# Two-layer-pair transformer in float32 on one Trainium2 core: residual with tokens on partitions, output projections with stationary tokens

## What is computed

```python
h = x
for layer in range(2):                       # first_block
    hn = rmsnorm(h, norm_mix_pre[layer])
    mix = gmlp_shortconv(hn, ...) if layer == 0 else dilated_attention(hn, ...)   # ends in @ w_out / @ w_o
    h = h + rmsnorm(mix, norm_mix_post[layer])
    f = square(relu(rmsnorm(h, norm_mlp_pre[layer]) @ w_up)) @ w_down             # 2048 -> 8192 -> 2048
    h = h + rmsnorm(f, norm_mlp_post[layer])
for layer in range(2):                       # second block
    hn = rms_norm(h, pre_norm_w[layer])
    mix = concat(diff_attention, sliding_window_attention, latent_attention)(hn @ w_in) @ w_out
    h = h + rms_norm(mix, post_norm_w[layer])
```

## Time and profile before

| | |
|---|---|
| Time, median of 3 runs | 3035.4 us (3034.12 to 3035.45) |
| The profiled execution's own time | 3034.49 us |
| Its span, first to last instruction | 3032.7 us |
| Mean granted clock of TensorE | 0.998 |
| PE busy | 3011.0 us, 99% |
| DVE, ACT, POOL busy | 71%, 48%, 10% |
| DMA | 549.49 MB, mean 181 GB/s, 50.3% of the 16 engines' time |

### The profile page before, as it was taken

The page is one execution under the profiler, slowest core; times in us unless marked ns, Lnnn a source line. Parts: engine busy times, 40 slices in busy tenths (PEclk is TensorE's granted clock), DMA queues, the critical chain, the costliest instruction groups (busy, mean ns, idle before and its releaser), DMA issues.

```text
span 3032.7 us, 42068 instructions
## 1 busy us (share of the span) xinstructions
PE 3011.0 (99%) x17482; PEld 2643.9 (87%) x17482; DVE 2167.7 (71%) x2878; ACT 1461.9 (48%) x1834; POOL 292.0 (10%) x191
## 2 busy tenths in 40 slices
PE   8999999999999999999999999999999999999999
PEld 7888888888888888888888888888888888888888
DVE  6776765767666687765856667676789865889764
ACT  5334534434334565445533334334666545656554
POOL 0003300000000410004100000002400003200003
PEclk9999999999999999999999999999999999999999
DMA  6555455555555444445455555555444445444445
GB/s 257 190 184 189 161 193 189 187 193 188 188 194 185 178 179 167 179 158 200 164 188 194 186 189 195 184 191 193 170 165 170 164 153 181 168 180 153 157 154 190
DMA packets 77500, 549.49 MB, mean 181 GB/s; under 512 B 8576, under 2 KB 9088, under 8 KB 11520
## 3 DMA queue, kind: packets, MB, share of 16 engines
q1 hardware_dynamic: 77312, 546.81, 50.3%
HBM read 544.68 MB, written 2.10 MB: 180 GB/s over the span
## 4 chain that ended last, share of the span: by engine, by line
PE 50%; DVE 2%; ACT 0%; issue 0%; DVEq 0%
PE acc L314 28%; PE acc L321 14%; PE score L546 1%; PE acc L839 1%; PE acc L364 1%; DVE w_low L1364 1%; PE head_out L575 1%; PE acc L846 1%; PE acc L374 1%; PE score L554 0%; PE acc L403 0%; PE acc L392 0%; PE extra L475 0%; ACT swapped L1049 0%; DVE y L1380 0%
## 5 line engine op out<-in xcount | busy, mean ns | idle before, releaser
L924 ACT ACTIVATE w_high<-raw 128x2048 fp32r<-128x2048 f32 x511 | 974.5, 1908 | 1109.8 <-DMA raw<-stream 1109.2
L1364 DVE TENSOR_TENSOR w_low<-raw,w_high 128x2048 fp32r<-128x2048 f32 (+1 forms) x509 | 1163.7, 2287 | 150.1 <-ACT w_high L924 147.1
L314 PE MATMUL acc<-xs,w_high 128*128 128x512 f32 x4444 | 1081.4, 394 | 0.6 <-ACT w_high L924 0.6
L314 PEld LDWEIGHTS acc<-xs,w_high 128*128 128x128 f32 x4444 | 819.6, 188 | 170.0 <-issue 6.9
L314 PE MATMUL acc<-inner,w_high 128*128 128x512 f32 x2880 | 679.9, 391 | 0.0
L314 PEld LDWEIGHTS acc<-inner,w_high 128*128 128x128 f32 x2880 | 532.7, 188 | 105.6 <-issue 0.7
L321 PEld LDWEIGHTS acc<-xs,w_low 128*128 128x128 f32 x4450 | 568.6, 192 | 17.0 <-issue 1.6
L321 PE MATMUL acc<-xs,w_low 128*128 128x256 f32 x4450 | 582.1, 283 | 1.3 <-DVE w_low L1364 1.3
L1380 DVE TENSOR_REDUCE y<-acc 128x256 f32<-128x512 f32 x374 | 258.0, 690 | 419.3 <-PE acc L321 247.0
L321 PEld LDWEIGHTS acc<-inner,w_low 128*128 128x128 f32 x2976 | 372.6, 191 | 9.7 <-issue 0.2
L321 PE MATMUL acc<-inner,w_low 128*128 128x256 f32 x2976 | 375.6, 283 | 0.1
(11 more groups left out here) (197 smaller groups left out, 1619.0 us busy)
## 6 DMA issues: line engine op xcount, KB each, us to landing
raw<-stream SPq DMA_DIRECT2D x514, 1024.0 KB, 4.8
out<-finished SPq DMA_DIRECT2D x8, 256.0 KB, 2.0
h<-x_t SPq DMA_DIRECT2D x3, 512.0 KB, 10.0
consts<-tables SPq DMA_DIRECT2D x1, 960.0 KB, 16.2
h<-x_t SPq DMA_DIRECT2D x2, 256.0 KB, 4.7
raw<-stream SPq DMA_DIRECT2D x2, 256.0 KB, 5.6
raw<-stream SPq DMA_DIRECT2D x1, 512.0 KB, 6.7
branch<-w_spatial SPq DMA_DIRECT2D x1, 512.0 KB, 17.0
```

Source lines behind the costliest of these rows:

```text
L314: return nc.tensor.matmul(acc[s if bank is None else bank][:, :], w_high[:, s, kt * P:(kt + 1) * P], x[:, kt, :, :], start=(kt == first_of ...
L924: nc.scalar.activation(w_high[:, s, 0:units * P], raw[:, s, 0:units * P], ACT.Copy)\
L1364: V.tensor_tensor(w_low[:, s, 0:units * P], raw[:, s, 0:units * P], w_high[:, s, 0:units * P], ALU.subtract).then_inc(low_ready, 1)
```

## The change

1. `h` and `branch` have tokens on partitions (`[P, TB, D]`). The input is loaded twice: features on partitions as `x_in` for the first sublayer, tokens on partitions into `h` later.
2. All output projections (`w_out`, `w_down`, `w_o`, 12 groups of 16 chunks, 192 chunks) and the first four chunks of both MLPs' up projections become wide chunks (`both_halves`, `one_half`, L377): stationary `inner` or `xs`, 512 moving weight columns. The last group of a sublayer ends with chunks 2 and 3 for the first 128 tokens, then for the second (`half_done` after the first).
3. Sums of squares run along the free dimension: ACT squares with an accumulator (`post_square`, `pre_square`). POOL only makes roots. The post gain is 512 columns of DVE (`out_gain`) with a gain row that SP loads, 4 pieces of 256 KB for each sublayer.
4. `turn_rows`: for each sublayer but the last 8 groups of 4 transposes by PE bring the new `h` back to features on partitions; ACT and DVE make `xs` from PSUM in pieces of 128 x 128 (`passage`). The next sublayer's first four chunks (`input_group`) follow the order in which they come (`TURNS`). In each MLP `turn_up` adds two groups of four.
5. `product_first`, `wide_first`, `parted`, `add_parts`, `product_last`, `product_low_first`, 17 `column_sums`, the 5 `spread`s of post-norm roots and the transposes at the end are gone. `h` is written out directly.

```diff
+TURNS = [(0, 0), (0, 1), (1, 0), (1, 1), (0, 2), (1, 2), (0, 3), (1, 3)]    # (half of the tokens, group of 4 blocks)
...
 # SP
+                for m, first in enumerate(OUTPUTS):
+                    g = c - 3 - first
+                    if 0 <= g < GROUPS:
+                        sp.dma_start(gain[:, wide_cols(g)], gains_post[m, :, wide_cols(g)])\
+                            .then_inc(sem(f"gain_landed_{g}"), 16)
...
 # PE
+            def one_half(c, i, n, x, banks, order=NATURAL, ready=None, hooks=None):
+                for k, (w, part) in enumerate(((w_high, 0), (w_high, 1), (w_low, 0))):
+                    pe.wait_ge(low_ready if w is w_low else high_ready, c + 1)
+                    for a in range(KT_WIDE):
+                        if hooks and KT_WIDE * k + a in hooks:
+                            hooks[KT_WIDE * k + a]()
+                        if ready and w is w_high:
+                            ready(KT_WIDE * i + a, part)
+                        mm = wide_unit(w, c % 4, x, order[KT_WIDE * i + a], a, part, n, banks[n], ...)
+            def turn_rows(m, k):
+                n, j = TURNS[k]
+                pe.wait_ge(sem("h_ready"), FINAL_GROUPS * m + k + 1)
+                if k > 2:
+                    pe.wait_ge(sem("xs_ready"), inputs_at(m + 1, k - 3))
+                for b in range(KT_WIDE):
+                    mm = nc.tensor.transpose(turn_banks[k % 3][:, b * P:(b + 1) * P],
+                                             h[:, n, (KT_WIDE * j + b) * P:(KT_WIDE * j + b + 1) * P], ident)
+            def input_group(c, n, banks, out0):
+                one_half(c, 0, 0, xs, banks, ready=first(0))
+                one_half(c + 1, 1, 0, xs, banks, ready=first(0), hooks={1: lambda: turn_rows(m, 2)})
+                one_half(c, 0, 1, xs, banks, ready=first(1), hooks={1: lambda: turn_rows(m, 3)})
+                one_half(c + 1, 1, 1, xs, banks, ready=first(1),
+                         hooks={4: lambda: turn_rows(m, 4), 8: lambda: turn_rows(m, 5)})
+                both_halves(c + 2, 2, xs, banks, ready=second,
+                            hooks={5: lambda: turn_rows(m, 6), 7: lambda: turn_rows(m, 7)})
+                both_halves(c + 3, 3, xs, banks, ready=second)
...
 # ACT, passage: high = rounding of a chunk, turn(k) = 4 copies of 128 x 128 to xs's high part
+                high(c, 0); last_sum(0); high(c + 1, 1); turn(0); turn(1); last_sum(1); turn(2)
+                high(c + 2, 2); pre_square(0); pre_square(1); turn(3); high(c + 3, 3); turn(4)
+                pre_square(2); turn(5); pre_square(3); high(c + 4, 0); turn(6); pre_square(4); turn(7)
...
 # DVE, passage: low = w_low of a chunk, add(k) = 512 columns of h, xs_low(k) = 4 of 128 x 128
+                low(c, 0); last_rows(0); add(0); add(1); xs_low(0); xs_low(1); last_rows(1)
+                add(2); low(c + 1, 1); add(3); xs_low(2); add(4); xs_low(3); add(5)
+                low(c + 2, 2); xs_low(4); add(6); xs_low(5); add(7); low(c + 3, 3); xs_low(6); xs_low(7)
```

More of the change, by code:

```diff
@@ L101, with inputs_before, build @@
 N_COLS = LAM_INIT + 2 * LAYERS
[L104 to L114, removed]
+def inputs_before(n):
+    return KB + TB * KB * (n - 1) if n else 0
+def build(nc, stream, x_t, x_rows, columns, gains_post, lambdas, w_spatial, b_spatial, positions, tables, out):
     ctx = ExitStack()
@@ new lines, in passage, with turn, pre_square @@
+            def passage(m, c, last_sum, gain_read):
+                def turn(k):
+                    n, j = TURNS[k]
+                    if j == GROUPS - 1:
+                        gain_read()
+                    act.wait_ge(sem("rows_turned"), FINAL_GROUPS * m + k + 1)
+                    for b in range(KT_WIDE):
+                        kt = KT_WIDE * j + b
+                        nc.scalar.activation(xs[:, kt, 0, rows(n)], turn_banks[k % 3][:, b * P:(b + 1) * P], ACT.Copy,
+                                             scale=column(G_PRE + KB * (m + 1) + kt)).then_inc(sem("xs_high"), 1)
+                def pre_square(k):
+                    n, j = TURNS[k]
+                    act.wait_ge(sem("h_ready"), FINAL_GROUPS * m + k + 1)
+                    act.wait_ge(sem("pre_squared"), FINAL_GROUPS * m + k)
+                    nc.scalar.activation(squares[:, :], h[:, n, wide_cols(j)], ACT.Square,
+                                         accum_out=pre_sums[:, n, j:j + 1]).then_inc(sem("pre_squared"), 1)
+                high(c, 0)
+                last_sum(0)
+                high(c + 1, 1)
+                turn(0)
+                turn(1)
+                last_sum(1)
+                turn(2)
+                high(c + 2, 2)
+                pre_square(0)
+                pre_square(1)
+                turn(3)
+                high(c + 3, 3)
+                turn(4)
+                pre_square(2)
+                turn(5)
+                pre_square(3)
+                high(c + 4, 0)
+                turn(6)
+                pre_square(4)
+                turn(7)
+                for k in range(5, FINAL_GROUPS):
+                    pre_square(k)
@@ L2087, in weight_stream @@
             blocks(w, part * width + P * j)
-    blocks(w_out_ab[0], 0, KB)
+    order = [r for b in MIX0_ORDER for r in range(P * b, P * (b + 1))]
+    for i in range(GROUPS):
+        wide(w_out_ab[0][order], WIDE * i)
     def mlp(layer):
         for q in range(FFN_QUARTERS):
-            blocks(w_up[layer], D * q, KB)
-            blocks(w_down[layer][D * q:D * (q + 1)], 0, KB)
+            if q == 0:
+                wide(w_up[layer], 0)
+                blocks(w_up[layer], WIDE, KB - KT_WIDE)
+            else:
+                blocks(w_up[layer], D * q, KB)
+            for i in range(GROUPS):
+                wide(w_down[layer][D * q:D * (q + 1)], WIDE * i)
     mlp(0)
@@ L2100, in weight_stream @@
                 blocks(w_qkv[0], D * part + P * hd)
-    blocks(w_o[0], 0, KB)
+    for i in range(GROUPS):
+        wide(w_o[0], WIDE * i)
     mlp(1)
@@ L2132, in weight_stream, with per_feature @@
         order += list(range(1536, D))
-        blocks(w_out_2[layer][order], 0, KB)
+        for i in range(GROUPS):
+            wide(w_out_2[layer][order], WIDE * i)
     return stream.reshape(LOADED, P, UNITS * P)
-def per_feature(sink_logits_2, gains_pre, gains_post, conv_w, q_norm, kv_norm, subln):
+def per_feature(sink_logits_2, gains_pre, conv_w, q_norm, kv_norm, subln):
     col = np.zeros((P, N_COLS), np.float32)
```

1032 lines of the change are left out of this document (454 added, 578 removed).

## The result

The changed kernel takes 3013.56 us (median of 4 runs, 3013.05 to 3015.66) beside 3034.76 us (3032.86 to 3035.45) for the kernel before on the same chip: a ratio of 0.9933, 95% interval 0.992 to 0.9945. It is faster by 0.7%. The forecast was 3020 us, range 3006 to 3033. The span of the profiled execution fell from 3032.7 to 3011.6 us, by 21.1 where the steps gave 15.4.

The account below looks back on a forecast made before the run. PE, busy 3011.0 of 3032.7 us, was taken as the bound. Terms -24 - 9.4 - 10.6 + 21 - 4.2 - 16.2 + 28 sum to -15.4 us, forecast 3020 us by the median, range 3006 to 3033.

Parts of the forecast that it names:

- (g): New passages between sublayers: PE waits for DVE and ACT, 5.2 us three times and 6.2 twice, +28 us.
- (d): Added PE transposes, 44 groups of four in `turn_rows` and `turn_up`, 0.48 us a group: +21 us.
- (f): Old PE waits at the passages go: 6.8 us into each MLP, 0.85 into three others, -16.2 us.
- (e): Kernel's end: last product to end falls from 11.5 to 7.3 us, half the rows leaving earlier, -4.2 us.
- (a): Projections and MLPs: 200 narrow chunks made wide, 5.44 instead of 5.56 us each, -24 us.
- (b): Products gone: double work of `parted` -8.2 us, short matmuls of six `product_last` -1.2 us.
- (c): 17 column sums and 5 spreads gone from PE's stream, 0.48 us a group, -10.6 us.
- Rival 5: Transposes run at the price of two-pass float32 matmuls: +15 us, 3035 us; chance 0.02.
- 1, the clock: PE's waits in the passages lower its clock, 8 us more each, 40 in all: 3060 us; chance 0.06.
- 2, the dearer passage: Passages cost about 9 us each without the clock, 45 in place of 28: 3037 us; chance 0.15.
- 3: Wide chunks bring nothing, (a) is 0: 3044 us; chance 0.04.
- 4, the better hidden passage: Overlap on DVE and ACT brings each passage to 2 to 3 us: 3006 us; chance 0.15.

Follow-up runs that it names:

- e1_short_pairs: Kernel before, with 16 matmuls of 256 columns in each narrow chunk's third pass made 8 of 512, same columns: 2989.17 us, ratio 0.9852.
- e15_sums_back: Changed kernel with 44 groups of two one-column sums, result unused, put among both MLPs' up products: 3034.27 us, 20.7 over the changed kernel.
- e4_no_unused_loads: Changed kernel without the three loads (3 MB) at the end of the stream that no product uses: 3010.79 us, ratio 0.992.
- e3_order: Changed kernel with the passage's DVE and ACT queues reordered, pieces PE waits for ahead of work that has time: 3005.38 us, ratio 0.9902.
- e13_whole_group: Changed kernel with each sublayer's last group not cut in halves and all its rows turned behind the last product: 3038.99 us, ratio 1.0015.
- e2_turn_twice: Changed kernel with each group of `turn_rows` transposes issued twice, 160 more transposes: 3022.43 us, ratio 0.9958 to the kernel before.

## Why the prediction was right

The mechanism was right, and the number partly by errors that cancel. The span fell by 5.7 us more than the sum said. The terms below come out 11.5 us cheaper ((g) 8, (d) 1.5, (f) 1.6, the start 0.4) and 3.9 us dearer ((e) 2.3, two sums 1.0, (a) 0.6), 7.6 in balance; the rest of 1.9, most of it as 0.4 to 0.8 in each of the three passages into a mixer, was not traced.

**(a) Chunks made wide: right.** -23.4 (12 groups of 16 at 1.87, of which six are measured alone in the middle of the MLPs, and 8 chunks at 0.117) for -24. e1_short_pairs gets the same 0.117 from the other layout, so the reason given, fewer matmuls for the same columns, is shown. The Trainium skill's rule for an isolated gap, columns / 2.4 + 2.5 ns ("TensorE: Matmul & The Clock Gate", section "Back-to-back issue gap"), would have made it an estimated -4; the section itself does not offer that rule for a stream, and these float32r matmuls in a stream start 226.7 ns apart, not 215.8. The prediction's "11 to 14 ns" over the columns' time is 13 to 14 by its own rows.

**(b), (c): right.** Neither `parted` nor a sum is left in the passages, and e15_sums_back measures 0.47 for the 0.48 a group. Two of the sums were counted twice, 1.0 us: they lay in the 11.5 us of (e). No run takes the double work of `parted` out alone.

**(d) Transposes: right, a little dear.** A group costs 0.36 and 0.08 to 0.1 behind it, 0.44 to 0.45 for 0.48, 1.5 us less in all. Rival 5 falls.

**(e) The end: mis-sized.** 9.6 us instead of 7.3. The chain was right (ACT's square 0.60 and 0.19 in place of 0.7, four adds in 2.74), the transfer was not: I took 2.1 us from the earlier trace rows, and it is 5.4 beside the last unused load. e4_no_unused_loads gives 2.1 and 7.0. The mean, 0.15 without a row, is 0.16. The prediction said that loads are no part of the passage and never asked about the loads at the end.

**(f) Waits of before: nearly right.** Two I had not looked for, 0.30 and 0.64 among the first narrow chunks behind `product_first` in each MLP (359.74 and 366.17 in the first), went as well (-1.9 together). The second MLP's idle stretch was 1.2 us shorter than the first's (1436.91 to 1441.50), but there the clock stood at 0.51 for 6 us of work instead of 4, about 0.9 us more lost, so 6.8 was 0.3 too much for it.

**(g) Waits of the new passage: right place, too dear.** About 3.3 us three times (the three waits named make 3.05 of it) and about 5 twice, 20 in all where I had 28. I put most of the surplus down to ACT and DVE on PSUM pieces, which no run isolates: four of 128 x 128 take 1.16 and 1.12 us, where I took 1.3 to 1.6 and 1.1 to 1.4, and a root 0.55 where I took 0.7. The timetable's waits add up to 4.6 and not to the 4.8 it says. It placed the third chunk's wait at 2.4 in sum and the fourth's at 1.65; they are 1.73 and 1.32. Its early waits of 0.25 and 0.3 do not exist in front of an MLP. Behind one they are 0.84 and 1.11 by the starts (0.68 and 0.95 in the brackets), where the timetable with 0.7 more for each has 0.95 and 1.0. That DVE's queue decides in front of the third chunk fits the rows of DVE above and e3_order, which takes `low` out of the way, reorders ACT a little too, and gets 8.2 us.

**Rivals.** 1, the clock: in all passages of the changed kernel it stays at full level, with waits of 1.5 us at most; e13_whole_group shows the danger to be real, since four of its five waits of 2.4 to 3.6 us are followed by a fall to 1.2 GHz. The Trainium skill says that a transpose does not count as PE-busy in the same way ("TensorE: Matmul & The Clock Gate", section "Part 4: PE-mode transpose"); eight groups of four among products, and eight groups of eight in e2_turn_twice, did not lower it in any passage. 2, the dearer passage: false, 4 us on the mean and not 9. 3: false. 4, the better hidden passage: true in direction, at 3.3 to 5 us and not 2 to 3. The time came out between the forecast's 3020 and its 3006.

**What I said would show it.** Wide chunks 5.44: yes. Transposes 0.09 us each, 160 of them: yes. Waits of 5 to 6 us in front of the third and fourth chunk: no, 3.05 into an MLP and 2.8 into the third sublayer, though ended by DVE and ACT as said. PEclk full: yes. 7 us at the end: only without the unused load. PE busy about 2990: 2979.

## What to carry to other kernels

Price a stream of matmuls by the distance of their starts in the trace, and count instructions as well as columns: here each, with its weight load, costs about 14 ns over its columns' time, and trading two of 256 columns for one of 512 was the whole gain in the projections. Where a chain between two stages can't be removed, cut the last stage so that half of the result is ready early. Then look at what stands ahead of the awaited pieces in the queues of the helping engines: moving the weights' `low` behind them was worth two fifths of the change again. At a program's end ask which transfers nobody waits for share the DMA engines with the output.

## What was not expected

- An idle stretch of 2.8 us on PE was followed by a fall of the clock and a loss of 1.7 us in the work behind it (0.51 over 330.5 to 334.0 in e13_whole_group); so was one of 2.44 us in the same kernel, and one of 2.45 was not.
- Outside the passages the clock can fall behind shorter waits, and not in every execution. In front of two groups of sums in the first sublayer PE waits 1.38 us in the changed kernel and 0.99 in e2_turn_twice, where the instructions up to this point are the same. Windows of the changed kernel and then of e2_turn_twice:

```profile
48.00:51.00 3.00, 3.00 (x14) 2.47 (x14) 1.09 (x2) 0.99 (x1) 1.76 (x2) 1.00 0.00 0
```

```profile
48.00:51.00 3.00, 3.00 (x9) 2.38 (x8) 0.45 (x2) 1.62 (x2) 1.75 (x2) 0.53 0.00 0
```

- The 256 KB writes at the end took 5.4 us (median) beside an unused 1 MB load and 2.1 us without it.
- Doubling the transposes cost half of their own time, since they ate a wait: 8.9 us for 17.4 us of work.
- The start of PE's first product varies between executions, 7.87 us in the profile of before, 6.83 in that of after and 6.2 to 7.0 in the others, e1_short_pairs with the old start among them (6.62); the 1.0 us between the two profiles is therefore not the change's.

Whether DVE could follow ACT piece by piece in `xs`, which would take the last 0.24 us in front of the third chunk, and whether the two waits behind an MLP (0.68 and 0.95) can be ordered away, was not tried.
